# A gated network with a filter: high weights meet both activation halves in one product, VectorE sums the halves

## The reference, cut to what matters

```python
def causal_dwconv(x, w): ...   # per column, over the rows t-2, t-1, t

def conv_glu_ffn(u, w_up, conv_w, conv_b, w_down):
    gu = u @ w_up
    gate = causal_dwconv(gu[..., :D_FF_2], conv_w) + conv_b
    return (jax.nn.silu(gate) * gu[..., D_FF_2:]) @ w_down
```

## Time and profile before

| | |
|---|---|
| median of 3 runs | 1324.52 us (1324.47 to 1324.85) |
| the profiled execution, its own time | 1324.93 us |
| its span in the trace | 1323.1 us |
| busy: PE, DVE, ACT | 1299.5, 972.6, 689.8 us |
| granted clock of TensorE over the span | 0.999 |

### The profile page before, as it was taken

One profiled execution on the slowest core, in us unless ns is written; L12 is line 12 of the kernel. 1 busy time (PEld: TensorE's weight loads), 2 busy tenths in 40 slices (PEclk: granted clock), 3 DMA queues, 4 the chain that ended last, 5 costly groups with the idle time before them and its releaser, 6 DMA issues.

```text
span 1323.1 us, 23114 instructions
## 1 busy us (share of the span) xinstructions
PE 1299.5 (98%) x9019; PEld 1182.7 (89%) x9032; DVE 972.6 (74%) x1537; ACT 689.8 (52%) x1077; POOL 100.8 (8%) x95
## 2 busy tenths in 40 slices
PE   7999999999999999999999999999999999999998
PEld 6888889998888888987999999899998888999997
DVE  6877777767687667787776666799897965766665
ACT  5444456666554443775544444677653544544442
POOL 1000000000000000120000000013102820000000
PEclk9999999999999999999999999999999999999999
DMA  8655545720356555414355555345431133555551
GB/s 302 213 205 189 190 168 176 255 96 1 134 200 214 189 189 190 144 60 150 137 196 187 190 190 191 132 171 176 160 112 51 65 104 138 205 191 190 190 191 64
DMA packets 30601, 214.83 MB, mean 162 GB/s; under 512 B 3648, under 2 KB 3776, under 8 KB 5184
## 3 DMA queue, kind: packets, MB, share of 16 engines
q1 hardware_dynamic: 30096, 212.23, 45.8%
q0 software_dynamic: 432, 1.57, 0.4%
HBM read 212.74 MB, written 1.05 MB: 162 GB/s over the span
## 4 chain that ended last, share of the span: by engine, by line
PE 89%; DVE 6%; ACT 3%; issue 2%; DMA 1%; POOL 0%; SPq 0%; POOLq 0%; DVEq 0%; ACTq 0%
PE bank L503 32%; PE bank L508 25%; PE bank L675 12%; PE bank L712 5%; PE bank L496 5%; PE bank L891 2%; DVE w_lo L2208 1%; PE bank L941 1%; PE bank L910 1%; ACT w_hi L1493 1%; DVE aT L2442 1%; PE bank L1132 1%; PE bank L561 1%; DMA raw<-weights 1%; PE bank L1367 0%
## 5 line engine op out<-in xcount | busy, mean ns | idle before, releaser
L2208 DVE TENSOR_TENSOR w_lo<-raw,w_hi 128x2048 fp32r<-128x2048 f32 x194 | 447.4, 2307 | 162.3 <-ACT w_hi L1493 161.9
L1493 ACT ACTIVATE w_hi<-raw 128x2048 fp32r<-128x2048 f32 x198 | 377.7, 1909 | 81.5 <-PE bank L712 46.5
L503 PE MATMUL bank<-aT,w_hi 128*128 128x256 f32 x1952 | 245.6, 284 | 0.0
L503 PEld LDWEIGHTS bank<-aT,w_hi 128*128 128x128 f32 x1952 | 239.7, 192 | 1.6
L508 PE MATMUL bank<-aT,w_lo 128*128 128x256 f32 x1664 | 216.3, 283 | 0.0
L508 PEld LDWEIGHTS bank<-aT,w_lo 128*128 128x128 f32 x1664 | 209.7, 192 | 3.4
L675 PE MATMUL bank<-aT,w_hi 128*128 128x512 f32 x688 | 164.8, 391 | 0.8 <-DVE aT L2235 0.7
L1563 ACT ACTIVATE arena<-arena 128x256 f32<-128x256 f32 x92 | 38.4, 418 | 230.4 <-DVE arena L2493 150.1
L503 PE MATMUL bank<-w_hi,hT_hi 128*128 128x512 f32 x400 | 156.5, 391 | 0.0
L508 PE MATMUL bank<-w_lo,hT_hi 128*128 128x512 f32 x400 | 151.9, 389 | 0.0
L675 PEld LDWEIGHTS bank<-aT,w_hi 128*128 128x128 f32 x688 | 127.2, 188 | 27.4 <-DVE aT L2235 1.4
(11 more groups left out here) (386 smaller groups left out, 1564.8 us busy)
## 6 DMA issues: line engine op xcount, KB each, us to landing
raw<-weights SPq DMA_DIRECT2D x198, 1024.0 KB, 4.9
post_gain<-post_gains POOLq DMA_DIRECT2D x3, 512.0 KB, 5.1
residual<-x SPq DMA_DIRECT2D x2, 512.0 KB, 4.0
raw<-weights SPq DMA_DIRECT2D x2, 512.0 KB, 7.2
out<-residual SPq DMA_DIRECT2D x2, 512.0 KB, 2.6
par<-params SPq DMA_DIRECT2D x1, 809.0 KB, 11.5
con<-consts SPq DMA_DIRECT2D x1, 520.0 KB, 11.1
con<-consts SPq DMA_DIRECT2D x1, 64.0 KB, 4.2
```

Of the source, the lines that this page charges most:

```text
L503: nc.tensor.matmul(to, lhsT, rhs, start=start and n == 0, stop=False)
L1493: nc.scalar.activation(w_hi[:, i % 3, :], raw[:, i % 3, :], ACT.Copy).then_inc(w_hi_done, 1)
L2208: nc.vector.tensor_tensor(w_lo[:, i % 3, :], raw[:, i % 3, :], w_hi[:, i % 3, :].bitcast(f32), ALU.subtract).then_inc(w_lo_done, 1)
```

## The change

glu1 and glu2 take the wide form of ff1 and ff2. Gate and up get a bank each and two pairs of banks take turns; before tile f PE waits until tile f-2 is summed. DVE sums (or, for tile 0, copies) gate and up into SBUF, ACT's scaling and DVE's filter read them there. ACT uses Silu in place of tanh and two steps of DVE. DVE's low splits move: with tile item i it now splits item i+2, in halves around the filter, and with a down item i again item i+2; in the last pair items 34 and 35 with tile 22, and 36 with tile 23. DVE takes the low part of a tile's hidden values later (with the next tile or the down item). ACT splits item i+3 ahead of Silu rather than behind tanh. Behind glu1's last tile ACT computes one Exp whose result isn't used. The taps, the down projection, ff1 and ff2 stay as they were; the buffer `f_tanh` becomes `f_silu`.

```diff
# PE, tile
-                    if not conv and f >= 2:
+                    if f >= 2:
                         pe.wait_ge(up_sum, f0 + f - 1 + 4 * q)
...
-                    if conv:
-                        to = [bank[4 + f % 4][:, 256 * part:256 * part + 256] for part in range(2)]
-                    else:
-                        to = [bank[4 + 2 * (f % 2) + part][:, 0:256] for part in range(2)]
+                    to = [bank[4 + 2 * (f % 2) + part] for part in range(2)]
...
+                            nc.tensor.matmul(to[part][:, :], w, aT[:, k, :, :].rearrange("p a c -> p (a c)"),
+                                             start=k == 0, stop=False)
...
+                            last = low_product(to[part][:, 0:256], weights(i, at, at + 128)[1], left(k), k == 7)
# ACT, tile
+                    act.wait_ge(gate_sum, f0 + f + 1 + 4 * q)
+                    late_split = f == n_tiles - 1
                     if conv:
...
-                        nc.scalar.activation(f_gate[:, f % 2, :], gate, ACT.Identity,
+                        nc.scalar.activation(f_gate[:, f % 2, :], f_silu[:, f % 2, :], ACT.Identity,
                                              scale=at_tile(tap, f, q, 2), bias=at_tile(bias, f, q))\
                             .then_inc(gate_scaled, 1)
+                        if not late_split:
+                            split(i + 3, 2 * q)
                         act.wait_ge(gate_conv, f0 - 44 + f + 1 + 4 * q)
...
+                        nc.scalar.activation(f_silu[:, f % 2, :], f_gate[:, f % 2, :], ACT.Silu).then_inc(gate_silu, 1)
...
                     act.wait_ge(hid_ready, f0 + f + 1 + 4 * q)
                     nc.scalar.activation(hT_hi[:, f % 4, :], f_hid[:, f % 2, :], ACT.Copy).then_inc(hid_hi, 1)
                     if late_split:
                         split(i + 3)
+                    if name == "glu1" and late_split:
+
+                        nc.scalar.activation(coef[:, 0, 0:1], half[:, 0:1], ACT.Exp)
# DVE
+                def low_part(f, q):
+                    dve.wait_ge(hid_hi, f0 + f + 1 + 4 * q)
+                    nc.vector.tensor_tensor(hT_lo[:, f % 4, :], f_hid[:, f % 2, :],
+                                            hT_hi[:, f % 4, :].bitcast(f32), ALU.subtract).then_inc(hid_lo, 1)
+
+                def sum_parts(f, i, q, gate_to, up_to):
+                    dve.wait_ge(item_done, i + 1 + 6 * q)
+                    if f == 0 and name in HALVED:
+                        nc.vector.tensor_copy(gate_to, bank[4][:, 0:256]).then_inc(gate_sum, 1)
+                        nc.vector.tensor_copy(up_to, bank[4][:, 256:512]).then_inc(up_sum, 1)
+                        return
...
+                def conv_tile(f, i, q):
+                    summed, hid, g = f_silu[:, f % 2, :], f_hid[:, f % 2, :], f_gate[:, f % 2, :]
+                    last = f == n_tiles - 1
+                    sum_parts(f, i, q, summed, hid)
+                    if f % 2 and f > 1:
+                        low_part(f - 1, q)
+                    if 0 < f and not last:
+                        split_half(i + 2, 0, r=2 * q)
+                    dve.wait_ge(gate_scaled, f0 - 44 + f + 1 + 4 * q)
+                    nc.vector.scalar_tensor_tensor(g[:, 1:256], summed[:, 0:255], at_tile(tap, f, q, 1),
+                                                   g[:, 1:256], ALU.mult, ALU.add).then_inc(conv_step, 1)
+                    dve.wait_ge(conv_step, f0 - 44 + f + 1 + 4 * q)
+                    nc.vector.scalar_tensor_tensor(g[:, 2:256], summed[:, 0:254], at_tile(tap, f, q, 0),
+                                                   g[:, 2:256], ALU.mult, ALU.add).then_inc(gate_conv, 1)
+                    if 0 < f and not last:
+                        split_half(i + 2, 1, r=2 * q)
+                    dve.wait_ge(gate_silu, f0 + f + 1 + 4 * q)
+                    nc.vector.tensor_tensor(hid, hid, summed, ALU.mult).then_inc(hid_ready, 1)
+                    if f < 2 or last:
+                        low_part(f, q)
+                    if f == n_tiles - 2:
+                        split(i + 3)
+                    if last:
+                        split(i + 3)
...
                 def down(m, i, q):
...
-                    if m < n_tiles // 2 - 1 - (name in BEHIND or name == "glu1"):
+                    if conv and m < n_tiles // 2 - 2:
+                        split(i + 2, 2 * q)
+                        low_part(2 * m + 3, q)
+                    elif not conv and m < n_tiles // 2 - 1 - (name in BEHIND):
                         split(i + 3, 2 * q)
```

More of the change, by code:

```diff
@@ L155, in two_blocks @@
         f_gate = room(2, SEQ)
-        f_tanh = room(2, SEQ)
+        f_silu = room(2, SEQ)
         f_hid = room(2, SEQ)
@@ L684, in tile @@
                             at = 1024 * part + 128 * k
-                            last = low_product(to[part], weights(i, at, at + 128)[1], left(k),
-                                               k == 7 and (part == 1 or not conv))
+                            last = low_product(to[part][:, 0:256], weights(i, at, at + 128)[1], left(k), k == 7)
                     last.then_inc(item_done, 1)
@@ L1556, in tile @@
                         tap, bias = tap.rearrange("p (f t) -> p f t", t=3), bias
-                        nc.scalar.activation(f_gate[:, f % 2, :], gate, ACT.Identity,
+                        nc.scalar.activation(f_gate[:, f % 2, :], f_silu[:, f % 2, :], ACT.Identity,
                                              scale=at_tile(tap, f, q, 2), bias=at_tile(bias, f, q))\
                             .then_inc(gate_scaled, 1)
+                        if not late_split:
+                            split(i + 3, 2 * q)
                         act.wait_ge(gate_conv, f0 - 44 + f + 1 + 4 * q)
[L1562 to L1566, removed]
+                        nc.scalar.activation(f_silu[:, f % 2, :], f_gate[:, f % 2, :], ACT.Silu).then_inc(gate_silu, 1)
+                    else:
+                        nc.scalar.activation(f_silu[:, f % 2, :], f_gate[:, f % 2, :], ACT.Tanh, scale=0.5)\
+                            .then_inc(gate_silu, 1)
+                        if not late_split:
+                            split(i + 3, 2 * q)
                     act.wait_ge(hid_ready, f0 + f + 1 + 4 * q)
@@ L2470, in ffn @@
                 tap = tap.rearrange("p (f t) -> p f t", t=3)
+                def low_part(f, q):
[8 more added lines that the diff above has]
+                        return
+                    sums = [bank[4 + 2 * (f % 2) + part] for part in range(2)]
+                    nc.vector.tensor_reduce(gate_to, sums[0][:, :].rearrange("p (a c) -> p c a", a=2), AX.X, ALU.add).then_inc(gate_sum, 1)
+                    nc.vector.tensor_reduce(up_to, sums[1][:, :].rearrange("p (a c) -> p c a", a=2), AX.X, ALU.add).then_inc(up_sum, 1)
@@ L2472, in tile @@
                 def tile(f, i, q):
-                    gate, up = bank[4 + f % 4][:, 0:256], bank[4 + f % 4][:, 256:512]
-                    g = f_gate[:, f % 2, :]
                     if conv:
[L2477 to L2496, removed]
```

22 lines of the change are left out of this document (11 added, 11 removed).

## The result

The changed kernel takes **1327.31 us** (median of 12 runs, 1324.49 to 1329.23), the kernel before 1324.60 in the same comparison (12 runs, 1324.24 to 1325.22): ratio 1.0022, 95% interval 1.0014 to 1.0029. It is slower, by 2.7 us; the forecast was 1.0 us faster. The forecast range, 1318.0 to 1327.5, holds the median, but only by 0.2 us, and the sign was wrong. The runs also spread over 4.7 us where those of before spread over 1.0. The profiled execution is the slowest of the twelve: 1329.23 us, span 1327.4.

A forecast was written before the change was run, and what follows sets the result against it. PE, busy 98% of the span, was taken to bound the kernel. Wide products -9.2, two network starts +6.2 and glu1's tail +1.95 gave -1.05 us: 1323.5 us forecast, range 1318.0 to 1327.5.

The forecast's parts named there:

- PE's part, a gain: Tiles 1 to 23 of glu1 and glu2: 16 products of 512 columns replace 32 of 256, 0.20 us a tile, -9.2 us.
- The start of each network, a loss: First tiles of glu1 and glu2: PE waits 0.35 us before tile 3, 2.75 in down item 4; +3.1 us a network.
- The tail of glu1: End of glu1: late last splits on DVE and ACT delay the transposes, +1.95 us, between 1.2 and 2.5.
- The loop at zero: Loops of glu1 and glu2: PE hides DVE's added work and the new bank wait, so no cost.
- Filter and scaling kept at the bank's price: Start timetable: DVE's filter (0.48) and ACT's scaling (0.56) keep their durations though now reading SBUF; 0.42 the other end.
- Sum. -9.2 + 6.2 + 1.95 = -1.05 us: Whole kernel: wide-product gain, two network starts and glu1's tail added, giving 1323.5 us.
- rival D: Down items after the new 2.75 us waits: clock falls to 1.2 GHz, +5 us a network, 1333.5; chance 0.03.
- A: Network starts: table load falls in ACT's idle time, waits shrink to 1.65, 1320.6, or vanish, 1317.3; chance 0.19.
- B: Loop: down item's low weights come late and each pair waits; at 0.25 us, 20 pairs lose 5.0, 1328.5; chance 0.08.
- C: Three new table loads on ACT each hold it for a second 1.28 us, 3.8 us in all, 1327.3; chance 0.06.
- E: glu1 and glu2 tiles: a wide product costs what two narrow ones do, 1332.7; chance 0.02.

The follow-up runs named there:

- the early table: Changed kernel, with one unused Silu on ACT ahead of tile 0 in glu1 and glu2, so its table loads early: 1322.29 us, ratio 0.9982.
- the tail's mend: Changed kernel, with item 35 split in halves around tile 23's filter and ACT's high part of item 36 ahead of tile 23's Silu: 1326.47 us.
- both mends: Changed kernel, item 4's low part whole behind tile 1's product, item 35 halved around tile 23's filter, item 36's high part before Silu: 1317.33 us.
- the narrow product: Fastest kernel measured (1316.13 us), with glu1's and glu2's wide product put back into two of 256 columns: 1325.55 us, ratio 1.0005.
- the start's mend: Changed kernel, with DVE making item 4's low part whole behind tile 1's product, not in halves with tile 2: 1319.03 us, ratio 0.9956.
- the best version: Changed kernel with item 4's early low split, glu1's end in halves with item 36's high part before Silu, and Silu's table loaded early: 1316.13 us.

## Why the prediction was wrong

**"PE's part, a gain", -9.2 us: right.** 9.4 measured by taking it back alone (9.2 against each one's own kernel before).

**"The start of each network, a loss", +3.1: right, a little small.** The waits shown are 0.37 and 2.45. Taken from start to start they are more: low products that normally hold PE for 1.91 us (688.05 to 689.96) held it for 2.44 (649.95 to 652.39), 0.53 more, and the stretch from 658.25 to 661.11 is 2.86 where 0.23 is usual, 2.63 more; the first products after each wait are 0.07 and 0.10 dearer (3.72 against 3.65 for the sixteen, 0.33 against 0.23). That is 3.33 a network: 0.16 to 0.18 us of each pause lies outside the idle time in the bracket. The timetable of glu1's start was within 0.2 us of every event.

**"The tail of glu1", +1.95: right**, 1.98. **The loop at zero: right.** **Filter and scaling kept at the bank's price:** right for the filter (0.48); the scaling became dearer (0.60), not cheaper.

**"Sum. -9.2 + 6.2 + 1.95 = -1.05 us": the step that failed,** because it has no term for the clock. The clock stood outside it as rival D, with a chance of 0.03, since the longest wait of before, 1.3 us, had not brought the clock down and since no row stood at the lower level. But that says nothing of the waits of 2.75 and 2.75 us that my own sum had just made, nor of the 2.2 us before the transposes, a place that D didn't name. The runs showed three falls. D's sign and its place at the starts were right, its price too high: not 5.0 us behind each start but 1.64 and 1.63 (1145.92 to 1152.32 is 6.40, against the 4.77). After glu1 it was 1.61: from the transposes (839.09, 841.39) to the next products at L503 it is 12.02 us before and 13.63 after:

```profile
851.11 4.07 PE L503 MATMUL bank<-aT,w_hi 128*128 128x256 f32 x32
```
```profile
855.02 1.19 PE L503 MATMUL bank<-aT,w_hi 128*128 128x256 f32 x8
```

With two unused products ahead of the transposes, and the clock at 1.00, it is 12.01 again (839.96 to 851.97).

The sum of the profiled execution then stands: 1324.93 - 9.4 + 2 x 3.33 + 1.98 + 4.88 = 1329.05, and 1329.25 with 9.2 for the wide product; measured 1329.23. That the range held the median all the same is luck: the working had no term that led from 1323.5 to 1327.3. In the median the clock is worth 3.0 us. That not every run has all three falls is inferred from the mean clocks, as only one execution was profiled: at 0.998 a run took 1324.49 us, at 0.995 four took 1328.79 to 1329.23.

The Trainium skill (TensorE: Matmul & The Clock Gate, "Why this matters for your kernels") warns of idle gaps between bursts. The trace agrees and goes further: the gaps of 2.2 to 2.5 us here are shorter than those that the section names. No profile here shows a fall behind the 1.3 us wait of the earlier trace rows. Had the sum taken D in at its three places and at the price measured here, it would have come to 1323.5 + 4.9 = 1328.4 with a fall each time; that price was not known then, and D's own would have given more.

**Rivals.** A failed, since the load stands right before its function; its price was right, as the early table showed (1.6 us waits). B failed: no wait in the loop. C failed: it is 1.29 us from load to function behind a split under way, so the 2.66 of the Trainium skill (ScalarE: Activation LUTs, "What ACT_TABLE_LOAD costs") isn't what these switches cost. That C's time, 1327.3, is the measured one is chance. E failed: the wide product is cheaper, as forecast.

**Still open.** What exactly brings the clock down. After glu1 it falls in profiles where PE idles only 0.8 us before the transposes (the tail's mend, both mends, the narrow product) and not in that of the start's mend, with 2.2 us, though it does in that of the early table, with the same 2.2. At the starts it falls behind 2.4 to 2.7 us and, in the profiles, not behind 1.6 or 2.0. The stretch after glu1 has a second gap (0.87 us before the first product of the projection), but all these kernels have it, the one before too, where the clock stayed at 1.00.

## What to carry to other kernels

Where PE bounds a loop, work moved from PE to another engine can pay in the loop and be paid back at its ends. Write out the first three tiles and the last pair engine by engine, and put first the split that the earliest reader wants (here item 4's, worth 8.3 us). Count an idle stretch of PE like those here (2.2 to 2.7 us) twice, once as the wait and once as the time that may follow at half clock (1.6 us each here); a spread of runs that wasn't there before was its sign in this case. Before a wait is judged harmless by the largest one in the trace of before, compare it with the largest one that the change itself makes.

## What the hardware showed that I had not expected

- The clock fell behind 2.2 to 2.5 us of idle PE, and the engine was then at 1.2 GHz for about 3 us at the starts and 6 to 7 after glu1. By the mean clocks of the runs this came in some executions of a kernel and not in others.
- A product of plain float32, 512 columns, ran as two passes, 0.86 us; in a wait of 2.4 us two of them kept the clock at 1.00, and five ended too late.
- Reading SBUF in place of a bank made ACT's scaling no cheaper: 602 ns against 564.
- An Exp whose result nobody uses was worth 1.6 to 1.8 us in the best version: without it a table load stands where PE waits for ACT (1.4 us).
